# Expert weights through six raw buffers instead of four in a two-block transformer kernel, with moved stores and row reads

## What is computed

```python
def moe_swiglu(h, router, w_gate, w_up, w_down):
    ...
    probs = jax.nn.softmax((ht @ router).astype(jnp.float32), axis=-1)
    vals, idx = lax.top_k(probs, TOP_K)          # 2 of 8 experts
    wts = vals / jnp.sum(vals, axis=-1, keepdims=True)
    ...
    for e in range(N_EXPERTS):
        out = out + gates[:, e:e + 1] * swiglu(ht, w_gate[e], w_up[e], w_down[e])
```

## Time and profile before

| | us |
|---|---|
| median of 3 runs (lowest, highest) | 1411.85 (1407.64, 1416.86) |
| the profiled execution, its own time | 1409.11 |
| its span in the trace | 1407.3 |
| mean granted TensorE clock | 0.985 |

### The profile page before, as it was taken

The page is one execution under the profiler, slowest core; times in us unless marked ns, Lnnn a source line. Parts: engine busy times, 40 slices in busy tenths (PEclk is TensorE's granted clock), DMA queues, the critical chain, the costliest instruction groups (busy, mean ns, idle before and its releaser), DMA issues.

```text
span 1407.3 us, 16215 instructions
## 1 busy us (share of the span) xinstructions
PE 1309.9 (93%) x6108; PEld 1079.0 (77%) x6108; DVE 945.4 (67%) x935; ACT 832.0 (59%) x896; POOL 34.3 (2%) x51
## 2 busy tenths in 40 slices
PE   6999999998788999999999999998889997999998
PEld 5888888887667787878787877776667775788886
DVE  4585555456757888888787878786956656555542
ACT  6445444357554777777777777676576455644431
POOL 3000000000001000000000000001010000000000
PEclk9999999999998999999999999999899999999999
DMA  9648664543136999999989898999774233355540
GB/s 305 211 155 282 204 204 158 178 132 136 64 132 230 372 352 370 343 396 342 390 338 391 331 387 336 383 347 374 253 268 171 87 124 116 119 186 176 207 151 31
DMA packets 90201, 342.33 MB, mean 243 GB/s; under 512 B 6235, under 2 KB 14128, under 8 KB 66480
## 3 DMA queue, kind: packets, MB, share of 16 engines
q1 hardware_dynamic: 87312, 330.87, 64.2%
q0 software_dynamic: 2816, 10.67, 2.2%
q10 hardware_dynamic: 16, 0.00, 0.0%
HBM read 334.18 MB, written 11.01 MB: 245 GB/s over the span
## 4 chain that ended last, share of the span: by engine, by line
PE 64%; DMA 11%; DVE 10%; ACT 8%; issue 5%; POOL 0%; ACTq 0%; DVEq 0%; SPq 0%
PE bank L1599 20%; PE bank L1601 19%; PE bank L1600 19%; DVE w_lo L327 6%; ACT w_hi L322 5%; DMA raw<-in_moe_w_up 4%; DMA raw<-in_moe_w_down 2%; DMA raw<-in_moe_w_gate 2%; DMA xT_lo<-moe_slots_out,row_from 1%; PE bank L1924 1%; PE bank L1699 1%; DMA moe_slots_out<-y 1%; ACT L322 1%; DVE e_act L1382 0%; PE bank L1682 0%
## 5 line engine op out<-in xcount | busy, mean ns | idle before, releaser
L327 DVE TENSOR_TENSOR w_lo<-raw,w_hi 128x2048 fp32r<-128x2048 f32 (+2 forms) x308 | 694.5, 2269 | 288.5 <-ACT w_hi L322 287.5
L322 ACT ACTIVATE w_hi<-raw 128x2048 fp32r<-128x2048 f32 (+2 forms) x308 | 582.8, 1901 | 314.4 <-PE bank L1601 217.2
L1599 PE MATMUL bank<-w_hi,xT_hi 128*128 128x512 f32 (+2 forms) x672 | 257.4, 383 | 13.7 <-issue 6.1
L1601 PE MATMUL bank<-w_hi,xT_lo 128*128 128x512 f32 (+2 forms) x672 | 254.7, 379 | 0.0
L1600 PE MATMUL bank<-w_lo,xT_hi 128*128 128x512 f32 (+2 forms) x672 | 254.5, 379 | 0.0
L1599 PE MATMUL bank<-w_hi,gT_hi 128*128 128x512 f32 x512 | 205.5, 401 | 26.3 <-DVE w_lo L327 22.3
L1600 PE MATMUL bank<-w_lo,gT_hi 128*128 128x512 f32 x512 | 201.4, 393 | 0.0
L1601 PE MATMUL bank<-w_hi,gT_lo 128*128 128x512 f32 x512 | 201.3, 393 | 0.0
L1599 PEld LDWEIGHTS bank<-w_hi,xT_hi 128*128 128x128 f32 x672 | 127.4, 190 | 38.4 <-issue 8.2
L1601 PEld LDWEIGHTS bank<-w_hi,xT_lo 128*128 128x128 f32 x672 | 127.5, 190 | 23.1
L1600 PEld LDWEIGHTS bank<-w_lo,xT_hi 128*128 128x128 f32 x672 | 127.5, 190 | 22.1
(11 more groups left out here) (374 smaller groups left out, 1239.1 us busy)
## 6 DMA issues: line engine op xcount, KB each, us to landing
raw<-in_moe_w_gate SPq DMA_DIRECT2D x64, 1024.0 KB, 6.2
raw<-in_moe_w_up SPq DMA_DIRECT2D x64, 1024.0 KB, 8.1
raw<-in_moe_w_down SPq DMA_DIRECT2D x64, 1024.0 KB, 6.2
raw<-in_w_gate_up SPq DMA_DIRECT2D x22, 1024.0 KB, 5.0
raw<-in_conv_w_in SPq DMA_DIRECT2D x12, 1024.0 KB, 9.3
raw<-in_ffn_w_gate SPq DMA_DIRECT2D x11, 1024.0 KB, 5.2
raw<-in_ffn_w_up SPq DMA_DIRECT2D x11, 1024.0 KB, 5.2
raw<-in_ffn_w_down SPq DMA_DIRECT2D x11, 1024.0 KB, 4.7
```

Source lines behind the costliest of these rows:

```text
L322: nc.scalar.activation(w_hi[:, slot, :n], raw[:, slot, :n], ACT.Copy).then_inc(stream.high, 1)
L327: nc.vector.tensor_tensor(w_lo[:, slot, :n], raw[:, slot, :n], w_hi[:, slot, :n].bitcast(F32), ALU.subtract).then_inc(stream.low, 1)
L1599: mm(dst, a_hi, b_hi, start=start, stop=False)
L1601: return mm(dst, a_lo, b_hi, start=False, stop=stop)
```

## The change

- The experts' chunks (`load_expert`) go through six raw buffers: the four of `raw`, rotated so that chunk 0 of the stage follows the chunk before it, and two in `raw_beside`. That tensor is laid over the place of `xT_hi` and `xT_lo`. Its first two loads wait for `moe_product`, the router's product, the last reader of the transposed tokens. All others wait for the low part of the chunk six before.
- `w_hi` and `w_lo` stay rings of four, and the splits run three ahead as before.
- The gathered rows land in a new tensor `back` (three blocks) and in `moe_g`, since the old place is a raw buffer now.
- On SyncE `store_rows` stands behind load c = 13 instead of c = 9, and `load_rows` behind c = 14 instead of c = 12. Expert 0 is a copy of its own there.
- The four `take_back` stand at c = 18 to 21 instead of 9 to 12.
- The second block's first four chunks wait for the low parts of chunks 18 to 21 of the last expert instead of 20 to 23.

```diff
+EXPERT_RING = RING + 2
...
         x = sb("x", [P, T, D])
+        with ExitStack() as inner:
+            raw_beside = inner.enter_context(nc.sbuf_tensor("raw_beside", [P, EXPERT_RING - RING, CHUNK], F32))
         xT_hi = sb("xT_hi", [P, KD, S], F32R)
...
+        def load_expert(c, e, first, view, k, n):
+
+            slot = c % EXPERT_RING
+            if first and c < RING:
+                nc.sync.wait_ge(W1.low, MOE0 + c - RING + 1)
+            elif first and c < EXPERT_RING:
+                nc.sync.wait_ge(sem("moe_product"), 1)
+            else:
+                nc.sync.wait_ge(W1.low, MOE0 + c - EXPERT_RING + 1 + EXPERT_CHUNKS * e)
+            nc.sync.dma_start(expert_raw[slot].rearrange("p (k n) -> p k n", k=k), view)\
+                .then_inc(expert_landed[slot], 16)
...
-        def returned(choice):
-            return (xT_hi, xT_lo)[choice].bitcast(F32).rearrange("p k s -> p (k s)")
+        def returned(choice, t):
+            at = choice * T + t
+            return M["back"][:, at, :] if at < 2 * T - 1 else M["moe_g"][:, :]
...
-                        load(MOE0 + c, e, W1, *expert_chunk(A, e, c, False))
-                        if c == 9:
+                        load_expert(c, e, first, *expert_chunk(A, e, c, False))
+                        if c == 13:
                             store_rows(e)
-                        if c == 12:
+                        if c == 14:
                             load_rows(e + 1)
...
-                            if c in (9, 10, 11, 12):
-                                take_back((c - 9) // 2, (c - 9) % 2)
-                                dve.wait_ge(sem("moe_taken_back"), c - 8)
+                            if c in (18, 19, 20, 21):
+                                take_back((c - 18) // 2, (c - 18) % 2)
+                                dve.wait_ge(sem("moe_taken_back"), c - 17)
```

More of the change, by code:

```diff
@@ L307, in build, with load @@
         W1, W2 = Stream("w1", first), Stream("w2", last)
-        def load(i, e, stream, view, k, n):
+        def load(i, stream, view, k, n):
             slot = i % RING
             if i >= RING:
-                nc.sync.wait_ge(stream.low, i - RING + 1 + EXPERT_CHUNKS * e)
+                nc.sync.wait_ge(stream.low, i - RING + 1)
             nc.sync.dma_start(raw[:, slot, :k * n].rearrange("p (k n) -> p k n", k=k), view)\
                 .then_inc(stream.landed[slot], 16)
+        expert_raw = [raw[:, (MOE0 + i) % RING, :] for i in range(RING)] + [
+            raw_beside[:, i, :] for i in range(EXPERT_RING - RING)]
@@ new lines, in build @@
+        expert_landed = [W1.landed[(MOE0 + i) % RING] for i in range(RING)] + [sem("expert_landed4"), sem("expert_landed5")]
+        landed_ahead = [len(range((MOE0 + i) % RING, MOE0, RING)) for i in range(RING)] + [0, 0]
+        def load_expert(c, e, first, view, k, n):
[8 more added lines that the diff above has]
+                .then_inc(expert_landed[slot], 16)
@@ L317, in split_high, with raw_of @@
+        def raw_of(i, stream):
+            if stream is W1 and i >= MOE0:
+                return expert_raw[(i - MOE0) % EXPERT_RING]
+            return raw[:, i % RING, :]
         def split_high(i, e, stream):
             slot, n = i % RING, stream.size(i)
-            nc.scalar.wait_ge(stream.landed[slot], 16 * (i // RING + 1) + 16 * (EXPERT_CHUNKS // RING) * e)
+            if stream is W1 and i >= MOE0:
+                c = i - MOE0
+                nc.scalar.wait_ge(expert_landed[c % EXPERT_RING],
+                                  16 * (landed_ahead[c % EXPERT_RING] + c // EXPERT_RING + 1) + 16 * (EXPERT_CHUNKS // EXPERT_RING) * e)
+            else:
+                nc.scalar.wait_ge(stream.landed[slot], 16 * (i // RING + 1))
@@ L320, in split_high @@
             if i >= RING:
                 nc.scalar.wait_ge(stream.used, i - RING + 1 + EXPERT_CHUNKS * e)
-            nc.scalar.activation(w_hi[:, slot, :n], raw[:, slot, :n], ACT.Copy).then_inc(stream.high, 1)
+            nc.scalar.activation(w_hi[:, slot, :n], raw_of(i, stream)[:, :n], ACT.Copy).then_inc(stream.high, 1)
         def split_low(i, e, stream):
@@ L326, in split_low @@
             nc.vector.wait_ge(stream.high, i + 1 + EXPERT_CHUNKS * e)
-            nc.vector.tensor_tensor(w_lo[:, slot, :n], raw[:, slot, :n], w_hi[:, slot, :n].bitcast(F32),
+            nc.vector.tensor_tensor(w_lo[:, slot, :n], raw_of(i, stream)[:, :n], w_hi[:, slot, :n].bitcast(F32),
                                     ALU.subtract).then_inc(stream.low, 1)
@@ L393, in _ @@
             for i, (_, view, k, n) in enumerate(first[:min(ENDS1, MOE0)]):
-                load(i, 0, W1, view, k, n)
+                load(i, W1, view, k, n)
                 if i == 1:
@@ L408, in load_rows, with expert @@
                         .then_inc(sem("moe_rows_loaded"), 16)
-                with sp.Fori(0, E - 1) as e:
+                def expert(e, first):
                     for c in range(EXPERT_CHUNKS):
-                        load(MOE0 + c, e, W1, *expert_chunk(A, e, c, False))
-                        if c == 9:
+                        load_expert(c, e, first, *expert_chunk(A, e, c, False))
+                        if c == 13:
                             store_rows(e)
-                        if c == 12:
+                        if c == 14:
                             load_rows(e + 1)
+                expert(0, True)
+                with sp.Fori(1, E - 1) as e:
+                    expert(e, False)
                 for c in range(EXPERT_CHUNKS):
-                    load(MOE0 + c, E - 1, W1, *expert_chunk(A, E - 1, c, True))
-                    if c == 9:
+                    load_expert(c, E - 1, False, *expert_chunk(A, E - 1, c, True))
+                    if c == 13:
                         store_rows(E - 1)
```

13 lines of the change are left out of this document (6 added, 7 removed).

## The result

| | before | after |
|---|---|---|
| median of 4 runs each, us (lowest, highest) | 1410.78 (1407.64, 1416.86) | 1369.82 (1367.83, 1370.6) |
| the profiled execution, us | 1409.11 | 1369.85 |
| its span, us | 1407.3 | 1368.0 |
| mean granted TensorE clock | 0.985 | 0.989 |

The ratio is 0.970 (95% interval 0.967 to 0.974): 41.0 us faster, where the forecast was 33.6. The measured time lies 0.2 us under the low end of the stated range. The last expert gained what was forecast; experts 0 to 6 gained more.

What follows compares the result with a forecast made beforehand. TensorE's work and its stalls were taken to bound the kernel; 16.4 + 4.0 + 13.2 = 33.6 us off 1411.85 gave 1378.2 us, with a range from 1370 to 1397.

Steps and rivals of the forecast that it cites:

- part 1: Experts 0 to 6: six raw buffers remove low-part waits and low clock, 16.4 us, and activation waits, 4.0 us.
- TensorE's own need: Experts 0 to 6: 507 us less 20.0 of stalls and 1.6 of low clock leaves 485.4, 69.3 us each.
- activation waits that the forecast held back: Experts 0 to 6: 8 TensorE waits for the activation, 5.2 us in all, of which 4.0 were taken as gain.
- the forecast's own lower case, 1371: Low end of the forecast, 1371 us: all 5.2 us of activation waits go, and chips differ.
- the allowance: Experts' raw chunks: time from a load's issue to its copy, 6.7 us with four buffers, 12.1 with six.
- the rate: Experts' transfers: 423 GB/s, seen over 18 us, would allow 62 us an expert, 64 with store and row read.
- Rivals 1 (full and half-way) and 3: Experts: transfers bind, 1398.6 us, half-way 1388 (0.09); deeper queue lowers the rate, 1431 us (0.04).
- rival 4: Experts: ring does not get ahead, SyncE waiting behind store or row read, 1398.6 us; 0.12 together with full rival 1.
- part 2: Last expert: the stall for gathered rows goes, 9.9 us, and the low clock behind it, 3.3 us; 13.2 us.
- reserve: Last expert: gathered rows would be there 12.5 us before VectorE wants them.
- Rival 2: Last expert: the gather comes too late again, leaving 20.4 us of gain, 1391 us; chance 0.05.
- cost nothing: Last expert: the four moved take-back steps, 1.28 us each, cost nothing; at most 5.1 us if their cover is gone.

Runs made afterwards that it cites:

- the ninth experiment: Changed kernel, loads waiting for the chunk four before, store and row read of experts 1 to 6 cut to one row of 128: 1399.0 us, ratio 0.992.
- the eighth experiment: Changed kernel without the product of the activations' high part with the weights' low part in the experts: 1325.05 us in a single run.
- sixth experiment: Changed kernel with store and row read back at c = 9 and 12, take_back left late: 1369.1 us, ratio 0.971.
- second experiment: Kernel before, four buffers, with store, row read and take_back moved to their new places: 1418.38 us, ratio 1.009.
- the fifth: Kernel before with take_back alone moved to c = 18 to 21: 1403.28 us, ratio 0.995.
- the fourth: Changed kernel, but each load waits for the low part of the chunk five before instead of six: 1375.19 us, ratio 0.977.

## Why the prediction was right or wrong

**The step that failed: the size of part 1.** The terms 16.4 + 4.0 = 20.4 us stood for experts 0 to 6; measured were 26.7. The forecast took 485.4 us as TensorE's own need, 69.3 an expert; it is 480.3 with the loop's end, 68.4 without it. So costs of the stalls were left in that need. Both traces list the same 312 matmuls for each expert in the same order, so the distance from each start to the next can be compared one by one:

| where before is longer than after | forecast, us | measured, us |
|---|---|---|
| the matmul that waited for a low part (13 waits forecast, 14 measured) | 14.8 | 15.1 |
| the low clock in expert 1 | 1.6 | 1.6 |
| the matmul that waited for the activation (8) | 4.0 | 5.2 |
| the next matmul behind each of these waits | 0 | 2.4 |
| a wait for ScalarE's `y` in expert 6 | 0 | 1.3 |
| all others, under 0.2 us each | 0 | 1.1 |

The fourth row is in the trace of before, after the stall of the earlier trace rows:

```profile
693.70 0.50 PE L1599 MATMUL bank<-w_hi,gT_hi 128*128 128x512 f32 x1 [1.38 <-DVE w_lo L327]
694.04 0.39 PE L1600 MATMUL bank<-w_lo,gT_hi 128*128 128x512 f32 x1
```

The next start comes after 0.34 us, not 0.23. Behind a wait for the activation the next transpose comes after 0.22 us, not 0.11. The fifth row is a wait for something else than the two that were summed, in expert 6:

```profile
871.20 0.50 PE L1599 MATMUL bank<-w_hi,gT_hi 128*128 128x512 f32 x1 [1.21 <-ACT y L810]
```

ScalarE's `y` stood there behind a split (868.26) that had waited for its raw chunk, and the wait went with the others. These two rows and the 1.2 us of activation waits that the forecast held back make 4.9 of the missing 6.3 us. The range's low end was then drawn from the forecast's own lower case, 1371. Of the way there only these 1.2 us had a cost behind them; the rest was put to differences between chips.

**Right in the allowance, wrong in what used it up.** TensorE's stalls came from raw chunks that landed late, and the splits behind them. The allowance of 4 x 2.72 - 4.2 = 6.7 us is borne out by the ninth experiment: without the store and the read, landings of 7.0 to 7.6 us still cause 3.0 us of loss an expert. With six, landings of up to 10.7 us in experts 1 to 6 (chunk 15 of expert 1) stay under the 12.1 allowed, and neither ScalarE nor TensorE waits for a chunk. In the last expert 13.7 us are over it, and TensorE still doesn't wait; that part the allowance doesn't explain. The forecast took the store and the row read for what makes chunks late, since 6.7 is "more than 4.7", the time of a load alone. But two or three chunks are under way at a time, and most of the loss, 3.0 of 3.8 us an expert, is there without store and read.

**Right: the rate.** (Of the seven experts before, one had 367 GB/s and a share of 0.97, a little above what the prediction names.) 423 GB/s over 18 us was a fair sign: the eighth experiment holds 411 to 422 over five experts. Rivals 1 (full and half-way) and 3 fall by this and by the 382 to 386 GB/s after, and rival 4 by the absence of any wait for a raw chunk. The Trainium skill, "DMA: Bandwidth & Descriptors", section "Where 436 GB/s comes from", lets the memory side bind at about 358 GB/s a core. These rows differ from it: the experts after the change run at 382 to 386 on the one core that the program uses. The Trainium skill, "HBM Reference", section "Specifications (TRN2)", gives about 425 for a core that streams alone, which the 423 and the 411 to 422 come near to.

**Right: the size of part 2,** 13.2 us against 13.3 measured, in both of its terms: matmul by matmul 9.9 us of waits went and 3.4 of late and slow starts behind them (9.9 and 3.3 forecast). Its reserve came out too, 12.5 us against 14.6. Rival 2, a gather that comes too late, didn't happen. Its neighbour did in two experiments: the gather delays the chunks rather than itself, to 12.9 us from issue to landing at a distance of five. With six, 0.8 us are left at chunk 17 and 0.3 at chunk 20. The forecast had no term for this and came out by luck of that margin.

**Half right: "cost nothing" for the moved steps.** Store, read and `take_back` were each costed at nothing beside the ring, and with six buffers that holds for store and read (sixth experiment). It doesn't for either half of the change by itself. In ratios to before:

| raw buffers | store, read at | take_back early | take_back late |
|---|---|---|---|
| four | 9, 12 | 1 | 0.995 |
| four | 13, 14 | | 1.009 |
| six | 9, 12 | 0.980 | 0.971 |
| six | 13, 14 | | 0.970 |

The interval of each ratio is 0.2 to 0.4% to either side. The later `take_back` is worth 0.5% with four buffers and 0.9% with six, which these intervals don't tell apart. The heap of store and read costs 1.4% with four and nothing with six. The moves alone lose 0.9%, the ring alone gains 2.0%, both together 3.0%: the parts don't add. Nothing that was run beats the changed kernel; the sixth, without the heap, is its equal.

## What to carry to other kernels

Size a ring by time, not by count: the distance in chunks times the consumer's pace, less the way from the consumer's release to the buffer's, should exceed the longest landing that occurs with the other loads under way, beside stores and gathers too, and not the one of a load alone; what is over it is paid from the consumer's lead. A high DMA share doesn't say that transfers bind; run the kernel with less compute, or find its fastest stretch. When stalls are summed from a waits view, take them from start to start over whole periods, and compare with an undisturbed period, since each stall brings costs that the view doesn't list. Judge a move of side traffic together with the ring's depth: the same move of store and read cost nothing at six buffers and 1.4% at four.

## What the runs showed of the hardware

- In the second experiment each of experts 0 to 6 has a wait of TensorE of 2.9 to 4.9 us from start to start, and in or behind it the granted clock falls to the lower level: 6 to 11 matmuls start 0.43 us apart instead of 0.23, 1.2 to 2.2 us on top (granted clock 0.84 on the mean of 690 to 712 us, which also holds the full-speed stretch before the wait). Seven such starts follow a wait of 2.33 us at 549.07 before; none follow one of 2.33 us at 550.55 in the fifth, one of 3.07 us at 964.98 in the fourth, or those of up to 2.0 us in experts 0 to 6 before and in the fifth. So idle time in one long piece often costs more than in several short ones, and these runs give no length from which it does.
- A chunk took 4.7 us alone, 7 to 10 with two to four under way, up to 13.7 beside and behind four gathers of 0.5 MB (chunk 21 of the last expert after: issued 953.94, landed 967.62), and none of this showed in TensorE's rows as long as the ring was deep enough.
- A store and a read of 0.5 MB each, issued one load apart, put 3.8 to 4.0 us between the landings of three successive chunks, where 2.5 is usual (second experiment, expert 3).
